# Attention outputs in three parts instead of one, on one Trainium2 core

## The reference

```
o_cmp = einsum("bgrsn,bngd->bsgrd", p_cmp, v_cmp)         # 31 compressed keys
s = q . k * scale + bias ;  p = masked_softmax(s)          # selected branch, window branch
o = g[:, :, 0] * o_cmp + g[:, :, 1] * o_slc + g[:, :, 2] * o_win
y = sigmoid(g_conv) * conv_out + sigmoid(g_attn) * nsa_out
```

## Time and profile before

| | |
|---|---|
| median of 3 runs | 2038.43 us (2036.83 to 2039.19) |
| the profiled execution | 2038.14 us |
| its span | 2036.3 us |
| mean granted clock of TensorE over the span | 0.987 |
| PE busy | 1899.3 us, 93% of the span |
| DVE, ACT, POOL busy | 751.0, 614.0, 633.4 us |
| the stage that the diff touches | 1304.7 to 1465.3 us of the span |

### The profile page before, as it was taken

One profiled execution on the slowest core, in us unless ns is written; L12 is line 12 of the kernel. 1 busy time (PEld: TensorE's weight loads), 2 busy tenths in 40 slices (PEclk: granted clock), 3 DMA queues, 4 the chain that ended last, 5 costly groups with the idle time before them and its releaser, 6 DMA issues.

```text
span 2036.3 us, 22123 instructions
## 1 busy us (share of the span) xinstructions
PE 1899.3 (93%) x8704; PEld 1223.9 (60%) x8704; DVE 751.0 (37%) x1548; ACT 614.0 (30%) x1115; POOL 633.4 (31%) x378
## 2 busy tenths in 40 slices
PE   5999988899999989989999899899899999999998
PEld 3544337633333333358888768644588578888886
DVE  5552265612222222252899305466421220000002
ACT  3112562311110110053124135366433342222213
POOL 0010432001110110054443234455443235546532
PEclk8999999989999999999999999999999999999999
DMA  9452013769999999953223421101132122322221
GB/s 394 170 208 84 35 36 114 300 279 418 428 427 428 427 427 428 427 201 120 108 83 97 131 83 53 62 22 32 63 114 85 40 93 83 115 93 83 106 101 62
DMA packets 89893, 359.33 MB, mean 176 GB/s; under 512 B 6939, under 2 KB 35995, under 8 KB 75212
## 3 DMA queue, kind: packets, MB, share of 16 engines
q1 hardware_dynamic: 86944, 352.80, 44.6%
q0 software_dynamic: 2304, 4.20, 0.6%
q10 hardware_dynamic: 556, 1.12, 0.1%
HBM read 356.46 MB, written 5.83 MB: 178 GB/s over the span
## 4 chain that ended last, share of the span: by engine, by line
PE 74%; DMA 14%; DVE 5%; ACT 3%; issue 2%; POOL 1%; SPq 0%; POOLq 0%; DVEq 0%; ACTq 0%
PE bank L750 14%; PE bank L752 14%; PE bank L751 14%; PE bank L725 11%; DMA slots<-in_w_expert_up 8%; PE bank L1129 7%; DMA slots<-in_w_expert_gate 4%; PE bank L1341 2%; PE bank L1361 2%; PE bank L881 2%; PE bank L1154 1%; PE bank L1330 1%; PE bank L1100 1%; ACT area L1933 1%; POOL low_r L2748 1%
## 5 line engine op out<-in xcount | busy, mean ns | idle before, releaser
L2748 POOL TENSOR_TENSOR low_r<-slots,high_r 128x2048 fp32r<-128x2048 f32 x82 | 379.1, 4625 | 523.5 <-ACT high_r L1571 523.4
L751 PE MATMUL bank<-xl_r,high_r 128*128 128x512 f32 (+1 forms) x832 | 322.0, 387 | 0.0
L750 PE MATMUL bank<-area_r,high_r 128*128 128x512 f32 x800 | 313.9, 392 | 6.1 <-POOL low_r L2748 6.1
L752 PE MATMUL bank<-area_r,low_r 128*128 128x512 f32 x800 | 312.2, 390 | 0.0
L1571 ACT ACTIVATE high_r<-slots 128x2048 fp32r<-128x2048 f32 x82 | 156.9, 1914 | 410.7 <-PE bank L752 404.3
L1129 PE MATMUL bank<-slots,area 128*64 128x512 f32 x992 | 229.8, 608 | 22.6 <-DMA slots<-in_w_expert_gate 15.6
L751 PEld LDWEIGHTS bank<-xl_r,high_r 128*128 128x128 f32 x832 | 157.8, 190 | 31.9 <-issue 0.5
L750 PEld LDWEIGHTS bank<-area_r,high_r 128*128 128x128 f32 x800 | 150.8, 189 | 38.0 <-POOL low_r L2748 6.3
L752 PEld LDWEIGHTS bank<-area_r,low_r 128*128 128x128 f32 x800 | 150.7, 188 | 31.4
L1129 PEld LDWEIGHTS bank<-slots,area 128*64 128x64 f32 x992 | 68.0, 139 | 168.4 <-issue 127.8
L2548 DVE SCALAR_TENSOR_TENSOR bank<-area,cols,bank 128x512 f32<-128x512 f32 x232 | 153.4, 747 | 0.0
(11 more groups left out here) (422 smaller groups left out, 2810.8 us busy)
## 6 DMA issues: line engine op xcount, KB each, us to landing
slots<-in_w_expert_down SPq DMA_DIRECT2D x32, 2048.0 KB, 16.5
slots<-in_w_expert_up SPq DMA_DIRECT2D x32, 2048.0 KB, 16.3
slots<-in_w_expert_gate SPq DMA_DIRECT2D x30, 2048.0 KB, 15.0
slots<-in_w_in SPq DMA_DIRECT2D x15, 2048.0 KB, 8.2
slots<-in_w_ada SPq DMA_DIRECT2D x11, 2048.0 KB, 12.2
slots<-in_ffn_in_w SPq DMA_DIRECT2D x22, 1024.0 KB, 6.6
slots<-in_ffn_out_w SPq DMA_DIRECT2D x5, 2048.0 KB, 7.8
slots<-in_w_out SPq DMA_DIRECT2D x4, 2048.0 KB, 7.8
```

The source lines that it names most:

```text
L750: nc.tensor.matmul(out, xh, yh, start=start and n == 0, stop=False)
L751: nc.tensor.matmul(out, xh, yl, start=False, stop=False)
L752: last = nc.tensor.matmul(out, xl, yh, start=False, stop=stop and n == len(pairs) - 1)
L2748: nc.gpsimd.tensor_tensor(low_half(m), raw_half(m), high_half(m), ALU.subtract).then_inc(s["w_low"], 1)
```

## The change

The outputs of a half-pair, one block on PE behind T(1) of the next, are cut by key tile into three parts: tile 0 (with the compressed keys in even half-pairs) behind T(1), tile 1 behind T(2), tiles 2 and 3 behind T(3). nsa_out is posted by the last part. DVE's nsa_keep_outputs moves one unit later, from u % 8 == 4 to u % 8 == 5. Matmuls, their shapes and their number stay the same. After the loop stand the last part of half-pair 14 and, in one block, all of half-pair 15.

```diff
-            def nsa_outputs(hb):
+            def nsa_outputs(hb, key_tiles):
...
-                if branch == 0:
+                if branch == 0 and key_tiles[0] == 0:
...
-                for a in range(2):
-                    pe.wait_ge(s[f"nsa_t_ready{a}"], 4 * hb + 4)
-                for j in range(TT):
+                if key_tiles[0] == 0:
+                    for a in range(2):
+                        pe.wait_ge(s[f"nsa_t_ready{a}"], 4 * hb + 4)
+                for j in key_tiles:
                     for a in range(2):
                         last = nc.tensor.matmul(bank[64 * a:64 * a + 64, j * P:C], VV[:, j, c0:c0 + 64],
                                                 PTN[hb % 2][a][:, j, j * P:C], start=False,
                                                 stop=(branch == 1 and j == TT - 1))
-                last.then_inc(s["nsa_out"], 1)
+                if key_tiles[-1] == TT - 1:
+                    last.then_inc(s["nsa_out"], 1)
...
                 if u >= 6 and u % 4 == 2:
-                    nsa_outputs(u // 4 - 1)
+                    nsa_outputs(u // 4 - 1, [0])
+                if u >= 6 and u % 4 == 3:
+                    nsa_outputs(u // 4 - 1, [1])
+                if u >= 8 and u % 4 == 0:
+                    nsa_outputs(u // 4 - 2, [2, 3])
             nsa_transposes(4 * NH - 1)
-            nsa_outputs(NH - 1)
+            nsa_outputs(NH - 2, [2, 3])
+            nsa_outputs(NH - 1, [0, 1, 2, 3])
...
-                if u >= 8 and u % 8 == 4:
+                if u >= 8 and u % 8 == 5:
                     nsa_keep_outputs(u // 8 - 1)
```

## The result

The changed kernel takes 2068.73 us (median of 4 runs, 2067.01 to 2069.55) against 2038.81 before: ratio 1.0143, 95% interval 1.0131 to 1.0156, 30 us slower. The forecast was slower, by 9 us. The profiled execution took 2069.27 us, its span 2067.4 us. Of the 31 us more in span than before, 29.8 lie in the stage of the change (1307.0 to 1497.4, 190.4 us against 160.6); what follows it takes 570.0 against 571.0 us, and what stands ahead of it 2.3 us more.

A forecast was written before the change was run, and what follows sets the result against it. A half-pair was taken as bound by a ring (outputs, S(1), T(2), S(2), T(3) on PE, then DVE, ACT, T(1)), not by PE. 2038.14 + 4.4 order + 4.8 clock = 2047.3, median 2047.5; range 2042 to 2051 us.

The forecast's parts named there:

- The ring and the stall: Half-pair ring PE, DVE, ACT, T(1): nsa_keep_outputs delays the copy of T(3), seven half-pairs 1.51 us longer, seven 0.75 shorter, +5.3.
- Changes of kind on PE: Two more switches between transposes and outputs per half-pair cost 0 to 0.6 us for 32; 0.2 taken.
- the end of the stage: Half-pair 14, from the start of its outputs to the last outputs: 4.25 us instead of 5.39, -1.1 us.
- The order alone: Sum for the stage without clock falls: +5.3 - 1.1 + 0.2 = +4.4 us.
- The clock: Granted clock falls to 0.50 after three of seven new thin PE stretches, 1.6 us each: +4.8 us, between 0 and 12.
- case 5: All or nearly all seven stalls bring a clock fall: +15.6 us, 2054; chance 0.05.
- Cover: Parts 2 and 3 (0.75 us) hide behind T(3): PE has 2.49 us to do in 2.83, 0.34 to spare.

The follow-up runs named there:

- place 6, rest behind T(3): Changed kernel with nsa_keep_outputs at u % 8 == 6, key tile 0 behind T(1) and tiles 1 to 3 together behind T(3): 2028.39 us, ratio 0.9944.
- place 6, two parts: Changed kernel with nsa_keep_outputs at u % 8 == 6, key tiles 0 and 1 behind T(1), 2 and 3 behind T(3): 2033.22 us, ratio 0.9970.
- place 6, three parts: Changed kernel with nsa_keep_outputs at u % 8 == 6 instead of 5, nothing else: 2037.7 us, ratio 0.9985.
- change, a quarter of the work: Changed kernel with both DVE instructions of nsa_keep_outputs cut to 128 of 512 columns: 2055.4 us, ratio 1.0065.
- one block, place 5: Kernel before, outputs still in one block, with nsa_keep_outputs at u % 8 == 5 instead of 4: 2062.37 us, ratio 1.0108.
- copy first: Changed kernel with nsa_keep_outputs still at u % 8 == 5 but behind DVE's copy of unit 3: 2058.33 us, ratio 1.0090.
- change, one filler: Changed kernel plus one 256-column filler matmul behind the scores of unit 0 in six of seven stalls: 2055.37 us over six runs, ratio 1.0080.
- change, three fillers: Changed kernel plus three filler matmuls a pair on PE in the long stall (512, 256 and 256 columns): 2048.75 us, ratio 1.0031.

## Why the prediction was wrong in size

| case | pair, clock up | S(3) to outputs, us | PE busy in it, us | stalls with a low stretch, of 7 |
|---|---|---|---|---|
| place 6, rest behind T(3) | 17.80 | 1.48 | 1.48 | 0 |
| place 6, two parts | 18.39 | 2.13 | 1.61 | 0 |
| place 6, three parts | 18.75 | 2.13 | 1.61 | 1, the seventh |
| before | 19.18 | 2.42 | 1.50 | 0 |
| change, a quarter of the work | 19.71 | 3.09 | 1.68 | 6 |
| one block, place 5 | 20.00 | 3.22 | 1.67 | 5 |
| copy first | 19.90 | 3.27 | 1.48 | 6 |
| change, one filler | 20.50 | 3.88 | 2.31 | 1, the seventh, without filler |
| change, three fillers | 20.51 | 3.89 | 3.65 | 0 |
| change | 20.5, from the fillers | 3.88 | 1.68 | 7 |

The columns of times hold for a stall among the first six, with the clock up. Place 5 or 6 is nsa_keep_outputs at u % 8 == 5 or 6. Each row is one profiled run; the change was profiled twice, with seven each time.

**The ring and the stall** were right. The two DVE instructions delay the copy of T(3), and PE waits where and for whom it was said; where they are moved off it, at place 6, the loss and the falls at the first six places are gone. The forecast of PE's waits was 1.17, 0.74 and 0.69 us; the profile shows 1.02, 0.56 and 0.62.

**Changes of kind on PE**, the places where it goes over from transposes to outputs or back, were mis-sized. The step "such changes cost 0.00 to 0.02 us ... I take 0.2" read a bound from the gaps between groups in the chain, and the cost does not show as a gap. In the profile after, from start to next start, part 1 takes 1.01 us (1402.92 to 1403.93 in a half-pair at full clock), part 2 0.79 (1405.42 to 1406.21) and part 3 0.80 (1408.08 to 1408.88), together 2.60 against 2.31 in one block. Parts 1 and 2, which stay on the ring, take 1.80 where the forecast had 2.31 - 0.75 = 1.56. The pair with the clock up costs 1.33 us more than before, not 0.76: the 0.57 between is 0.28 a half-pair, 4.0 us over seven pairs. At the end of the stage the three-filler kernel is 0.9 us shorter than the kernel before (9.46 against 10.36 us from the last start of L1355 to wo2) where 1.1 was forecast. The order alone costs 7 x 1.33 - 0.9 = 8.4 us instead of 4.4. Two parts against three show the same kind of cost from outside: 0.18 us for each change of kind taken away.

**The clock** was the step that failed: "Of the seven new stretches I take three ... I take 1.6". All seven fell, in both profiles of the change, and each cost 3.0 us, since the low clock lasted 6.8 us and not the 3.4 of the earlier trace rows. That is 21.4 us instead of 4.8, and it is over two thirds of the stage's 29.8. My case 5, all stalls with a fall, had a chance of 0.05 and came to 2054 with falls of half the length.

The number of falls was counted from four stretches of one profile, two that fell and two that did not. The new stretch was thinner than both neighbours at 1458 and 1508, and the fallen one at 1605 was nearest to it; I counted that one as one case among four. But the four rows were a weak ground in any case. Three of these stretches lie outside the changed stage and come back unaltered in the profile of the change, and there each came out the other way. Windows, PE alone: the stretches that stood at 1508 and 1605, each with what follows it, then the gap that stood at 1658, with what follows:

```profile
1541.07:1545.06 3.99, 2.49 (x17) 1.00 0.66 194
1545.06:1549.00 3.94, 3.92 (x33) 1.00 0.90 342
1637.76:1640.51 2.75, 0.44 (x3) 1.00 0.00 0
1640.51:1645.00 4.49, 3.70 (x8) 1.00 0.00 0
1689.46:1692.88 3.42, 0.00 (x1) 1.00 0.65 193
1693.44:1696.85 3.41, 3.41 (x18) 0.50 1.09 361
```

Over the twelve profiles of this case the clock fell behind these three in 5, 8 and 9. So "the one at 1658 shows that even a gap of 3.42 us need not bring a fall" is right, but the profile it was read from was one of only three in which that gap brought none. Nor are the stalls independent draws, as three of seven would have it: in the one-block, the quarter and the copy-first kernel the first one or two stalls kept the clock, and every stall behind the first fall had one. Why a fall makes the next likely, no run shows.

The length was missed because each row showed PE back at dense work before the fall; here it fell while the stall still lasted or just at its end (1341.86, with T(1) at 1342.95; 1413.54, with T(1) at 1413.26), and it stayed low for twice as long. The other kernels bear this out. Of the 33 low stretches by a stall in all profiles, the 25 of 6.8 us began between 1.1 us ahead of the start of T(1) and 1.0 us behind it, the 8 of 3.4 us between 1.2 and 2.2 us behind it.

The Trainium skill's section "HAM oscillation — how this bites in real kernels" of "TensorE: Matmul & The Clock Gate" warns by idle gaps. No single wait in the stalls of the change passed 1.02 us, apart from 1.67 in the seventh, and the clock fell all the same; where the Trainium skill and the trace differ, the trace decides. The Trainium skill says in "Part 1: The HAM clock gate (the "warmup" mystery)" of "TensorE: Matmul & The Clock Gate" that the gate follows how busy PE has been recently. The two filler kernels agree with that: three fillers left no fall, one filler none in the six stalls that had it in the one run profiled. What exactly a stretch must lack for a fall stays open.

**Cover.** The forecast that parts 2 and 3 hide behind T(3) holds: wait for ACT's copy 0.62 to 0.20 us, for the bias pass 0.30 to none. Its last step could have led to a better kernel: with 0.34 us to spare, part of key tile 1 (0.64 us) hides there too, and the kernel with tiles 1 to 3 behind T(3) gained another 0.30 us a half-pair over two parts.

## What to carry to other kernels

When a change makes a producer later, look at what its consumer's instruction is queued ahead of: here 1.4 us of DVE work, hidden at one place of the loop, delayed a link of the ring at the next one and cost nothing at the one after. Price a new stall on PE twice, once as time and once by what PE does in and around it; if the whole stretch is as thin as one after which the clock fell, reckon with a fall at every turn, and a low clock on the dense work behind it. Do not take the chance of a fall from one profile: the same instructions kept the clock in one and lost it in the next, so look for the stretch in several. Work that leaves a ring in fewer, larger pieces gains more than the same work in many.

## What the runs showed that was not expected

More matmuls made a kernel faster: 256 useless columns in each of six stalls took the change from a ratio of 1.0130 to 1.0080, 1024 columns in six and 768 in the seventh to 1.0031. Between the kernel before, with 2.42 us from S(3) to the outputs, and the quarter kernel with 3.09, PE's longest wait in the first six stalls stays at 0.62 and 0.63 us, and the falls go from none to six of seven; in the seventh stall of the kernel before a wait of 1.42 us brought none. A low stretch by a stall came in two lengths, 3.4 and 6.8 us, and which one followed how far PE was past the stall when the clock fell. And a change between transposes and outputs on PE costs some 0.14 to 0.18 us for blocks as small as these, though neighbouring starts in the trace show no idle time.
